# A front of 32 modulation units: float32 products in four column groups, and the first dense units in quarters between them

## The reference

```
mod_lat = silu(c) @ w_ada + b_ada          # w_ada: 2048 x 6144, float32
mod_ctx = silu(c_ctx) @ w_ada + b_ada
shift, scale, gate = split(mod, 3)
u_l = rms_norm(x, pre_w)   * (1 + scale_l) + shift_l
u_c = rms_norm(ctx, pre_w) * (1 + scale_c) + shift_c
p = u @ w_in                               # z, xbc, dt, q k v, beta, alpha for all 512 tokens
```

## Time and profile before

| | |
|---|---|
| runs shown | 3125.22, 3140.85, 3168.91 us |
| median | 3140.85 us |
| profiled execution | 3152.78 us, span 3151.0 us, mean granted clock 0.994 |
| TensorE busy | 3066.9 us |
| VectorE, ScalarE, GpSimd busy | 1921.2, 1378.0, 182.6 us |
| moved by DMA | 544 MB, mean 173 GB/s |

### The profile page before, as it was taken

One profiled execution on the slowest core, in us unless ns is written; L12 is line 12 of the kernel. 1 busy time (PEld: TensorE's weight loads), 2 busy tenths in 40 slices (PEclk: granted clock), 3 DMA queues, 4 the chain that ended last, 5 costly groups with the idle time before them and its releaser, 6 DMA issues.

```text
span 3151.0 us, 68364 instructions
## 1 busy us (share of the span) xinstructions
PE 3066.9 (97%) x28654; PEld 2866.2 (91%) x28654; DVE 1921.2 (61%) x2547; ACT 1378.0 (44%) x1751; POOL 182.6 (6%) x281
## 2 busy tenths in 40 slices
PE   6899999999999999999999999999999999999999
PEld 1477777788898999999999999999999999999999
DVE  6766666668886666655555555566665554555544
ACT  5545445445445445444333333444444333333332
POOL 0000000000010000211000000200002110000000
PEclk9999999999999999999999999999999999999999
DMA  8612112122494444555555555554445555555554
GB/s 342 265 68 82 69 69 81 70 81 102 190 350 161 174 173 173 187 189 198 188 199 188 199 188 197 202 189 175 171 170 180 185 185 187 186 186 187 187 187 146
DMA packets 79937, 544.00 MB, mean 173 GB/s; under 512 B 8325, under 2 KB 12437, under 8 KB 15392
## 3 DMA queue, kind: packets, MB, share of 16 engines
q1 hardware_dynamic: 76272, 519.08, 45.8%
q10 hardware_dynamic: 2768, 19.66, 1.6%
q0 software_dynamic: 736, 2.90, 0.3%
HBM read 537.38 MB, written 4.22 MB: 172 GB/s over the span
## 4 chain that ended last, share of the span: by engine, by line
PE 88%; DVE 5%; issue 4%; ACT 2%; DMA 0%; POOLq 0%; DVEq 0%; ACTq 0%; POOL 0%
PE bank L428 27%; PE bank L429 26%; PE bank L430 26%; DVE w_lo L412 2%; PE bank L757 1%; ACT w_hi L407 1%; PE bank L643 1%; PE bank L678 1%; PE bank L687 1%; DVE s_acc L1507 0%; PE bank L1036 0%; PE bank L857 0%; DVE g_L L1660 0%; PE bank L637 0%; PE bank L840 0%
## 5 line engine op out<-in xcount | busy, mean ns | idle before, releaser
L407 ACT CAST w_hi<-raw 128x2048 fp32r<-128x2048 f32 x477 | 910.5, 1909 | 1301.5 <-PE bank L430 1268.3
L412 DVE TENSOR_TENSOR w_lo<-raw,w_hi 128x2048 fp32r<-128x2048 f32 x477 | 1097.4, 2301 | 574.9 <-ACT w_hi L407 574.3
L428 PE MATMUL bank<-a_lo,w_hi 128*128 128x256 f32 (+1 forms) x3664 | 1099.6, 300 | 12.6 <-DVE w_lo L412 10.1
L429 PE MATMUL bank<-a_hi,w_lo 128*128 128x256 f32 (+1 forms) x3664 | 1073.5, 293 | 0.0
L430 PE MATMUL bank<-a_hi,w_hi 128*128 128x256 f32 (+1 forms) x3664 | 1072.9, 293 | 0.0
L428 PE MATMUL bank<-h_lo,w_hi 128*128 128x256 f32 x3584 | 1005.3, 280 | 0.8
L429 PE MATMUL bank<-h_hi,w_lo 128*128 128x256 f32 x3584 | 995.3, 278 | 0.0
L430 PE MATMUL bank<-h_hi,w_hi 128*128 128x256 f32 x3584 | 995.0, 278 | 0.0
L428 PEld LDWEIGHTS bank<-a_lo,w_hi 128*128 128x128 f32 x3664 | 694.7, 190 | 37.9 <-DVE w_lo L412 12.2
L430 PEld LDWEIGHTS bank<-a_hi,w_hi 128*128 128x128 f32 x3664 | 691.2, 189 | 19.8
L429 PEld LDWEIGHTS bank<-a_hi,w_lo 128*128 128x128 f32 x3664 | 691.1, 189 | 15.5 <-issue 0.5
(11 more groups left out here) (330 smaller groups left out, 1937.9 us busy)
## 6 DMA issues: line engine op xcount, KB each, us to landing
raw<-stream SPq DMA_DIRECT2D x485, 1024.0 KB, 4.8
gate_raw<-stream ACTq DMA_DIRECT2D x16, 1024.0 KB, 6.8
xr<-x_t SPq DMA_DIRECT2D x4, 1024.0 KB, 16.4
turned<-by_distance POOLq DMA_DIRECT2D x1, 2048.0 KB, 11.0
x_res<-x_t SPq DMA_DIRECT2D x1, 2048.0 KB, 17.3
bias_table<-bias SPq DMA_DIRECT2D x1, 2048.0 KB, 11.2
bias<-bias_table ACTq DMA_DIRECT2D x1, 2048.0 KB, 10.4
out_t<-x_res SPq DMA_DIRECT2D x4, 512.0 KB, 5.1
```

Source lines behind the costliest of these rows:

```text
L407: act.copy(w_hi[u.slot][:], raw[u.raw][:]).then_inc(hi_ready, 1)
L412: dve.tensor_tensor(w_lo[u.slot][:], raw[u.raw][:], w_hi[u.slot][:], ALU.subtract).then_inc(lo_ready, 1)
L428: pe.matmul(acc, wh, lo[:, k, 0:n], start=(k == first), stop=False)
L429: pe.matmul(acc, wl, hi[:, k, 0:n], start=False, stop=False)
```

## The change

1. No modulation unit is split. Each is four float32 products, as the native ones were, but contraction tile t goes to column group t: stationary 128 x 32 (`c32`: two columns of c and c_ctx and 30 of zeros), output partitions 32t to 32t + 31, accumulated over the four units of a group. The row copy now takes 128 partitions, and the selecting matrix adds the four groups. SyncE waits for `unit_done` of a modulation unit before it reuses its buffer.
2. Units SMALL, GDN 0, 1 and 2 come as four quarters m. A quarter is one buffer of 1 MB in pieces of 2 KB: contraction tiles 4m to 4m + 3 of all four units. They stand at places 12, 20, 27 and 33 of now 36. ScalarE and VectorE split a quarter in two halves of 1024 columns each. TensorE issues it in four parts j (one unit each; 12 instructions) behind modulation units 13 to 16, 21 to 24 and 28, 29, and the rest behind unit 31. The four units accumulate over that time in banks 0, 1, 2 and 4 (`Unit.bank`), so the small chain uses bank 5 where it had 2 and 4.
3. GDN 3 comes after the small chain's sums and rows, as before; its split moves to the end of quarter 2. The split of GDN 4 moves from behind padded(1) to behind the copies of rows (ScalarE), and to behind the chain (VectorE).
4. Clearings on VectorE (six of 128 x 128) go; their semaphores are counted up by clearings that GpSimd does anyway. Column copies for the SSD tiles (8 small ones) move into the first head, behind `u32_set`. The masks are requested behind the last shifts instead of behind the squares.

```
+QUARTER_AT = (12, 20, 27, 33)
+QUARTER_AFTER = {13: (0, 0), 14: (0, 1), 15: (0, 2), 16: (0, 3), 21: (1, 0), 22: (1, 1), 23: (1, 2), 24: (1, 3),
+                 28: (2, 0), 29: (2, 1)}
...
+        self.bank = {U_GDN + 1: 2, U_GDN + 2: 4}.get(self.n, c % 2) if isinstance(self.n, int) else c % 2
+        self.slot = (c - U_SMALL) % SPL
+        self.split = self.n - FIRST + 1
...
+            def free(p):
+                kind, m = FRONT[p]
+                if kind == "ada":
+                    sp.wait_ge(unit_done, m + 1)
+                else:
+                    sp.wait_ge(S["q_lo"], 2 * m + 2)
+            def quarter(m, r):
+                row = stream_row(U_SMALL)
+                sp.dma_start(d3(raw[r][:], D // QUARTERS), stream[row:row + 4, :, m * D // QUARTERS:(m + 1) * D // QUARTERS]
+                             .rearrange("a p m -> p a m")).then_inc(raw_ready[r], 16)
...
-            pool.wait_ge(S["ss1"], 1)
+            pool.wait_ge(S["shift_set"], PAIRS)
             pool.dma_start(masks[:], const_dram[:, KEEP:N_CONST]).then_inc(S["ld_masks"], 16)
...
+            def modulation(p, n):
+                g, q = n // 4, n % 4
+                pe.wait_ge(raw_ready[p % RAW], (p // RAW + 1) * 16)
+                for t in range(4):
+                    m = mm(psum[6 + g % 2][t * B32:(t + 1) * B32, :], c32[:, (q * 4 + t) * B32:(q * 4 + t + 1) * B32],
+                           raw[p % RAW][:, t * 512:(t + 1) * 512], start=(q == 0), stop=(q == 3), skip_group_check=True)
                 m.then_inc(unit_done, 1)
...
+            def quarter(m, j, i0=0, i1=4):
+                slot = m % SPL
+                pe.wait_ge(S["q_lo"], 2 * m + j // 2 + 1)
+                u = Unit(U_SMALL + j)
+                n = L if j == 1 else T
+                acc = psum[u.bank][:, 0:n]
+                for i in range(i0, i1):
+                    k = 4 * m + i
+                    if j == 0:
+                        pe.wait_ge(S["u_ready"], k + 1)
+                    wh, wl = (w[slot][:, (j * 4 + i) * P:(j * 4 + i + 1) * P] for w in (w_hi, w_lo))
+                    pe.matmul(acc, wh, u_lo3[:, k, 0:n], start=(k == 0), stop=False)
+                    pe.matmul(acc, wl, u_hi3[:, k, 0:n], start=False, stop=False)
+                    last = pe.matmul(acc, wh, u_hi3[:, k, 0:n], start=False, stop=(k == KT - 1))
...
+            done = 0
+            for p, (kind, n) in enumerate(FRONT):
+                if kind == "ada":
+                    modulation(p, n)
+                    if n == RAW + 1:
                         squares()
+                    if n // 4 > done:
+                        to_columns(done)
+                        done += 1
+                    if n in QUARTER_AFTER:
+                        quarter(*QUARTER_AFTER[n])
+            quarter(2, 2, 0, 2)
+            to_columns(done)
+            quarter(2, 2, 2, 4)
+            quarter(2, 3)
+            for j in range(3):
+                quarter(3, j)
+            quarter(3, 3, 0, 2)
             pe.wait_ge(S["sm_beta"], 1)
+            turn(5, [sm_e[:, c * P:(c + 1) * P] for c in range(C)]).then_inc(S["sm_turned"], 1)
+            quarter(3, 3, 2, 4)
...
-            first_unit(2)
-            first_unit(3)
+            unit_mm(pe, Unit(U_GDN + 3), u_hi3, u_lo3, L)
...
+            act.copy(d3(c32[:], B32)[:, :, 0:2], d3(cs[:], 2)).then_inc(S["cols_set"], 1)
...
+            modulation_row(0)
+            act.wait_ge(S["ss1"], 1)
+            root(rs1[:], psum[4][:], ln1[:], 1.0 / D, "rs1_ready")
+            for m in range(QUARTERS):
+                modulation_row(2 * m + 1)
+                for k in range(4 * m, 4 * m + 4):
                     high(k)
+                if m == 0:
+                    modulation_row(2)
+                    quarter_high(0)
+                elif m == 1:
+                    quarter_high(1)
+                    modulation_row(4)
+                elif m == 2:
+                    quarter_high(2)
+                    modulation_row(6)
+                    quarter_high(3)
+            act.wait_ge(S["q_done"], QUARTERS - 1)
+            split_act(act, Unit(U_GDN + 3), True)
             act.wait_ge(S["sm_lin"], 1)
...
+            square_sum()
+            dve.wait_ge(S["rs1_ready"], 1)
+            for m in range(QUARTERS):
+                coefs(m)
+                for k in range(4 * m, 4 * m + 4):
+                    scaled(k)
+                if m == QUARTERS - 1:
+                    quarter_low(m, 0)
+                    quarter_low(m, 1)
+                shifts(m)
+                for k in range(4 * m, 4 * m + 4):
+                    low(k)
+                if m < QUARTERS - 1:
+                    quarter_low(m, 0)
+                    quarter_low(m, 1)
```

More of the change, by code:

```diff
@@ L77 @@
 GATE_ROW = 32
-NATIVE = tuple(n for n in range(U_SMALL) if n % 4 == 2)
-SPLIT = [n for n in range(U_SMALL + SPL) if n not in NATIVE]
+QUARTERS = 4
+FIRST = U_SMALL + QUARTERS
+QUARTER_AT = (12, 20, 27, 33)
+FRONT, _next = [], 0
+for _p in range(FIRST):
+    if _p in QUARTER_AT:
+        FRONT.append(("quarter", QUARTER_AT.index(_p)))
+    else:
+        FRONT.append(("ada", _next))
+        _next += 1
+QUARTER_AFTER = {13: (0, 0), 14: (0, 1), 15: (0, 2), 16: (0, 3), 21: (1, 0), 22: (1, 1), 23: (1, 2), 24: (1, 3),
+                 28: (2, 0), 29: (2, 1)}
 CONST = {"ident": 0, "ones": P, "flip": 2 * P, "blk": 3 * P, "sel": 4 * P}
@@ L135, in constants @@
     for r in range(4):
-        out[r, CONST["sel"] + r % 2] = 1.0
+        for v in range(2):
+            out[r * B32 + v, CONST["sel"] + v] = 1.0
     for d in range(2):
@@ L516, in _ @@
                              x_dram[r * 512:(r + 1) * 512, :].rearrange("(k p) t -> p k t", p=P)).then_inc(ld_x[r], 16)
[L517 to L520, removed]
+            for p in range(RAW, FIRST + RAW):
+                free(p - RAW)
+                kind, n = FRONT[p] if p < FIRST else ("unit", p)
+                (quarter if kind == "quarter" else load)(n, p % RAW)
+            for begin, end in ((FIRST // RAW + 1, U_BC // RAW), ((U_LAYER + 12) // RAW, N_SEQ // RAW)):
                 with sp.Fori(begin, end) as i:
@@ L669, in to_columns @@
                     at = ada_group(g) * 8 + j * 2
-                    m = mm(psum[3 + 2 * (g % 2)][:, at:at + 2], mrow[g % 2][0:4, j * P:(j + 1) * P], K("sel", 0, 2)[0:4, :],
+                    m = mm(psum[3 + 2 * (g % 2)][:, at:at + 2], mrow[g % 2][:, j * P:(j + 1) * P], K("sel", 0, 2),
                            start=True, stop=True)
                 m.then_inc(S["ada_cols"], 1)
[L674 to L679, removed]
-                m.then_inc(unit_done, 1)
@@ L682, in halves @@
-            def halves(u, out, q):
-                for w, ready in ((w_hi, hi_ready), (w_lo, lo_ready)):
-                    pe.wait_ge(ready, u.split)
-                    for k in range(4):
-                        m = mm(out[0:4, :], c4[:, (q * 4 + k) * 4:(q * 4 + k) * 4 + 4], w[u.slot][:, k * 512:(k + 1) * 512],
-                               start=(q + k == 0 and w is w_hi), stop=(q * 4 + k == 15 and w is w_lo))
-                m.then_inc(unit_done, 1)
-            for g in range(2 * PAIRS):
-                for q in range(4):
-                    u = Unit(4 * g + q)
-                    (native if u.n in NATIVE else halves)(u, psum[6 + g % 2], q)
-                    if u.n == RAW + 1:
-                        squares()
-                    if q == 2 and g:
-                        to_columns(g - 1)
@@ L1104, in padded @@
                 if split:
-                    split_act(act, v.ahead(2))
+                    split_act(act, v.ahead(split))
             def silu(i, k, j):
@@ L1158, in head @@
                         m.then_inc(S["ut_ready"], 1)
-                        padded(u.ahead(4), 2, False)
+                        padded(u.ahead(4), 2, 0)
                     else:
```

162 lines of the change are left out of this document (58 added, 104 removed).

## The result

The changed kernel takes 3101.9 us (median of 20 runs), the kernel before 3132.6 in the same number of runs. The ratio is 0.9906, 95% interval 0.9886 to 0.9926: 29 us gained by the ratio and 31 by the medians, where 37.5 were forecast. The two profiled spans differ by 55 us.

A forecast was written before the change was run, and what follows sets the result against it. TensorE was busy 97% of the span, but the front was a loop of buffer, cast, subtraction and products close to DMA. 186.2 - (111 + 37.7) = 37.5 us gained, off 3140.85: 3103 us; 3084 to 3131 for 8 in 10.

The forecast's parts named there:

- the term for the bubbles: Gaps in DMA during the front, from buffers requested late: 4 us added to the arrival of the last modulation unit.
- Modulation units: Four float32 products per unit in four column groups, near full overlap: 0.95 us a unit, between bounds 0.9 and 3.6.
- DMA rate and the 2 KB pieces: Front loads move at 409 GB/s, and quarters coming in pieces of 2 KB cost nothing.
- Tail: From the last modulation unit's landing to the first head's Gram products: 37.7 us, with VectorE next on the path.
- D: Time at which the last modulation unit lands: 111 us, bounds 107 and 125.
- the meeting point: Start of the first head's Gram products, 186.24 us before; everything gained ahead of it was taken as gained at the end.
- the 107 of the sum: Landing of the last modulation unit without bubbles: 5 us, then 41.7 MB at 409 GB/s, giving 107 us.
- It just fits: Behind units 13 to 16, 14.6 us of TensorE work against 10.2 of arrival: lag 4 to 5, with 5.5 allowed.
- the one for bubbles: Sign of being wrong: DMA holes behind units 13 to 16, 21 to 24 and 28.
- The clock did fall to 0.50: Rival: TensorE stays at 1.2 GHz in the front and needs 124 us; gain 12, 3128 us; chance 10%.
- Column groups taking turns: Rival: each modulation unit's four products cost 3.6 us instead of 0.95; 10 us late, 3151 us; chance 6%.
- The front stays fed at no more than 335 GB/s: Rival: request order or 2 KB pieces hold DMA down; last modulation unit at 129 us, gain 19, 3122 us; chance 12%.

The follow-up runs named there:

- e3: Changed kernel with the four products of each modulation unit sent to one column group, one after the other; 3147.3 us, ratio 1.0045.
- e11: Changed kernel without 9 of 12 products in each part of quarters 0 and 1, splits of quarters 1 and 2 ahead of the shifts; 3080.7 us.
- e6: Changed kernel with the parts of quarters spread out between modulation units and the splits of quarters 1 and 2 ahead of the shifts; 3099.7 us.
- e9: Changed kernel without 9 of 12 products in each part of quarters 0 and 1, all loads, splits and orders kept; 3082.6 us.
- e10: Changed kernel with the parts of quarters spread out and unread products added where TensorE idles, splits in their old place; 3084.8 us.
- e5: Changed kernel with 3 to 10 unread float32 products added behind units 7 to 12, 17 to 19 and 25 to 27, where TensorE idles; 3109.5 us.

## Why the prediction was right, and which term was off

- **The number.** The time was forecast as 3103 and measured as 3101.9 us. That this is so close is luck: the forecast started from a median of three runs, 3140.85, 8 us above the median of 20, and took off a gain that was 7 to 8 us too large. The path was right, a front bound by DMA and a tail behind it, and so was the size of the tail; the term for the bubbles was not.
- **Modulation units.** Forecast 0.95 us each. Measured at full clock: 0.88 from start to start where two stand in a row and 1.0 with a part's product behind; 1.86 at half clock. Right, and e3 shows that overlap is the cause. The Trainium skill, "TensorEngine Tiling (Array Packing)", section Theoretical Speedup, gives up to 4 times for 32 columns; e3 against the changed kernel is 3.9 to 4.0 (3.48 us against 0.88). The change of tiling mode costs what was assumed, 0.1 us: a unit starts 0.32 us behind the last product of a part (69.18 to 69.50), where products of a part follow each other by 0.23.
- **DMA rate and the 2 KB pieces.** Right: 400 to 426 GB/s in every window from 5 to 60 us with quarter 0 in it, 409 from 60 to 109 us in e11 with the three other quarters.
- **Tail.** From D, the landing of unit 31, to the meeting point 37.7 us were forecast. Measured are 39.6, of which the first 2.0 are TensorE's lag behind the landing (118.8 to 120.8). From its start on unit 31 they are 37.6. The transposes, forecast for D + 16, came 15.9 us behind that start; the wait ahead of the Gram products was on VectorE, as said. The masks held up nothing.
- **D.** The term that was mis-sized, the bubbles: forecast were 4 us behind the 107 of the sum, measured 11.8 (landing at 118.8), and 13.8 until TensorE starts the unit (120.8, where 111 was forecast). These 9.8 us are the whole difference between 37.5 and the 27.9 at the meeting point. The step "It just fits" failed, in three ways. First, it asked only how late TensorE frees the buffers of modulation units. It did not follow the quarter's own buffer, which is freed at the end of a chain over turn, shifts, high, low and split. Quarter 2's was free 10.9 us after its landing, where 5.5 were allowed, and the next load took 4.8. The wait was in the diff, behind the instructions that stand ahead of `quarter_low` on VectorE. Second, the stretch from unit 13 to the end of part (0, 3) was put at 14.6 us, for a warm start, and took 18.1 (56.3 to 74.4), since unit 13 and the first part ran at 1.2 GHz (the part from 58.15 to 62.95, 4.8 us and not 2.8). So the lag behind the arrival was 8 us and not 4 to 5. Third, TensorE came out of each hole at 1.2 GHz: the products behind the one at 100 to 105 us were 0.43 us apart. Of the prediction's own signs of being wrong, the one for bubbles came true, with holes behind units 13 to 16 and 21 to 24.
- **Rivals.** The clock did fall to 0.50, with units of 1.93 us from 28.7, 52.6, 82.9 and 108.7 us on, but holding it at 1.00 from 45 us on brought 0.9 us at the meeting point; it adds to a lag, it doesn't make one. Column groups taking turns was priced as 10 us slower than the kernel before; e3 is 11 later at the meeting point and 16 by the medians. For "The front stays fed at no more than 335 GB/s" the mean rate came out near it for 45 to 125 us (343), but not its D of 129, and with another cause than was named: requests held up by engines, not pieces or a limit of DMA.
- **The meeting point** was the right measure for the front: 27.9 us there, 29 by the ratio. It isn't all of the time: e6 and e9 both meet at 153.2 and their medians are 17 us apart (last section).

## What to carry to other kernels

In a ring of buffers that one queue fills in order, follow each buffer to what frees it, all of the chain over all engines, and set it against the landings still in flight; here one buffer with another kind of release held up all behind it. Work put under a transfer has to be spread at the pace of the transfer, since a burst delays what feeds the ring even where the sum has room. When two causes hide behind each other, removing either shows less than half of it (3.5 and 5.2 of 12.4 us here), and a run without both, even one that computes less, shows the whole. And a forecast time that comes true says little while the gain in it is off: check the gain, term by term.

## What was unexpected of the hardware

The last layer ran at one of two paces. Windows of 100 us, two of the kernel before and then two of the changed one:

```profile
2350.00:2450.00 100.00, 100.00 (x849) 99.89 (x848) 55.31 (x52) 41.48 (x38) 20.63 (x31) 1.00 0.53 188
2700.00:2800.00 100.00, 100.00 (x851) 100.00 (x850) 53.35 (x52) 39.17 (x34) 9.85 (x16) 1.00 0.54 189
```

```profile
2350.00:2450.00 100.00, 100.00 (x865) 99.89 (x864) 55.68 (x54) 41.42 (x38) 16.96 (x26) 1.00 0.52 188
2700.00:2800.00 100.00, 100.00 (x885) 100.00 (x884) 52.32 (x46) 38.71 (x28) 5.53 (x9) 1.00 0.54 193
```

TensorE is fully busy and its clock is granted in full in all four, but from 2700 to 2800 us 851 products of 256 columns start in one and 885 in the other: 117.5 ns apart against 113.0. The code is the same. Both kernels begin the layer at the slow pace; the changed one turns to the fast pace near 2400 us (2430 of the kernel before, the same product), the kernel before never does, and 27 us lie between them at the end. In e11's profile the pace is the slow one, in e9's, with the same layer, the fast one. What sets it isn't known.

In the first heads the distance between two kernels moves in steps of about 3.6 us, where the granted clock of one of them dips below 1.00 in a window of 20 us. The gain over the kernel before falls from 27.9 to 21.5 us over the changed kernel's dips (0.89 at 160 to 180 us, 0.91 at 180 to 200, and this one):

```profile
230.00:250.00 20.00, 18.01 (x498) 13.45 (x497) 9.48 (x19) 5.53 (x17) 0.00 (x0) 0.91 0.20 71
```

It rises again to 28.6 over those of the kernel before:

```profile
370.00:390.00 20.00, 18.02 (x499) 13.46 (x498) 9.20 (x18) 5.52 (x17) 0.00 (x0) 0.92 0.21 79
430.00:450.00 20.00, 17.79 (x479) 13.22 (x480) 9.44 (x19) 5.52 (x17) 0.00 (x0) 0.96 0.29 109
```

The dips fall on different heads in different kernels, and they are what the medians show beyond the front. At the Gram products of the eighth head e9 is 15 us ahead of e6, which met it at 153.2 (558.9 against 574.1), and e10 is 12 us ahead of the changed kernel, 5 of them from the front. e5 is 1 us ahead of the changed kernel at the meeting point and 7 behind it there. What decides where the clock dips is not shown. The dips make one profile's end, and a median too, a worse measure of the front than the meeting point.
